# Part of the last projection block moved between attention's first scores, with a new instruction order for the attention stage

## Chip, cores and metric

The kernel runs on one core of one Trainium2 chip. A core has TensorE (PE), VectorE (DVE), ScalarE (ACT), GpSimd (POOL) and SyncE (SP), which issues most DMAs. The metric is device microseconds of one launch; less is better.

## What is computed

One inference step of a decoder with two layers, for a prompt of 1024 tokens and 8 x 4 = 32 sample tokens, 1056 in all, width 1024, in float32. Layer 0 projects x to 3352 columns that feed two branches. Layer 1 is a pooling mixer. The change touches layer 0 alone, cut here to what matters:

```python
h = jnp.einsum('btd,de->bte', x, w_in)
a_val, a_glu, a_gate, q, kv_c, kv_s, kv_w, g, b_gate = jnp.split(h, offsets, axis=-1)
u = a_val * jax.nn.sigmoid(a_glu)
# branch A: causal depthwise convolution of width 31, layer norm over channels, gates
a_out = jax.nn.silu(layer_norm(y, ln_g, ln_b)) * jax.nn.silu(a_gate)
# branch B: attention over compressed blocks, the 16 best blocks and a window of 512
o = gq[..., 0:1] * o_c + gq[..., 1:2] * o_s + gq[..., 2:3] * o_w
h = jnp.concatenate([a_out, b_out * jax.nn.silu(b_gate)], axis=-1)
y = jnp.einsum('bte,ed->btd', h, w_out)
x = layer_norm(alpha * x + y)
```

The 32 sample tokens attend to 2048 cached keys each, fetched page by page, and their block choice depends on their compressed scores.

## The kernel before

**Projection.** `one(m)` computes block m of 27 (m = 0 to 26), 128 columns of `w_in` for all tokens. Weights are loaded to WRAW, split by ACT into a high part WH (`high`), and by DVE or POOL into the rest WL (`low`). PE makes 72 matmuls of 352 columns per block (line 728): 8 slices of the contraction, three products (XH with WH, XL with WH, XH with WL), three column thirds. `evac(m)` on ACT takes the result out of three PSUM banks, 0 to 2 for even m, 3 to 5 for odd. Block 22 holds the attention gates G, blocks 23 to 26 the quarters of `b_gate` (BG), with a SiLU.

**Statistics.** The layer norm of branch A runs beside blocks 24 and 25. `mean(c)` and `variance(c)` (lines 763 to 772) are matmuls of PE with a constant matrix, put between the block's slices; DVE centres, adds squares and normalises (lines 648 to 677), ACT squares and takes the root, and afterwards applies SiLU to Y (line 494). POOL then multiplies Y by the gate AG (line 357). Before block 24 PE transposes the gates G (line 836), which ACT copies to GTOK (line 483).

**Values.** After block 26 PE transposes the value rows of KV (lines 852 and 858), and ACT and DVE copy them to TM (lines 501 and 680).

**Attention.** For each of 48 units (query tile, head pair, branch) there are two pairs p: `S` scores on PE (line 1334) into banks 0 to 3, `M` masks and takes the least on DVE (line 1432), `E` is the exponential on ACT (line 1377), `R` the reciprocal on DVE (line 1428), `C` the scaling on POOL (line 1589). `T` are turns of the probabilities by PE into banks 4 and 5 (line 1195), which DVE and ACT copy to PT (lines 1367 and 1371), and `V` multiplies them by the values into bank 6 (line 1213). `H` and `cast` split Y for the output product (lines 1533 and 1617).

**Samples.** One bank, 7, serves the samples' steps one after another: `csc`, compressed scores (line 1226); `cmax`, `cexp`, `cnorm`; `gs`, sums over heads (line 1234), from which `rank` on DVE chooses blocks (lines 1463 to 1469); `kt`, turned key tiles (line 1251); `sc` and `scw`, scores (line 1257), taken by DVE; `pt` and `pv`, the values' product (line 1310). Selected keys come by gathers of POOL's queue into RING (line 1574), window rows by SP's queue (line 1621). `dve_queries` fills QBD, `pool_prep` and `dve_prep` the small columns TI, NEWM, NM4 and WM4.

**Order.** The order of all this on each engine comes from a planner that runs when the program is built. It holds a list of steps with durations and lags in ns, simulates them, and takes at each point the step with the largest remaining path plus a constant per engine and kind:

```python
begin = max([now[e] + (SWITCH if mode != pe_mode and e == "PE" else 0)] + [end[y] + lag for y, lag in after])
may.append((begin, remains[x] + PREFER.get((e, kind), 0), kind, x))
```

Of the kernel before, what the change touches and what calls it, by code (L numbers as in the profile page):

```python
# [72 lines left out]
def program(nc, x_prompt, x_sample, cache_kv_cmp, cache_kv_sel, state_win_kv, state_conv, state_pool, page_table,  # L73
# [4 lines left out]
    with ctx:  # L78
# [61 lines left out]
        EPSC = const("EPSC", [P, 1])  # L140
        assert cur[0] <= 206016 + 6368, cur[0]
# [48 lines left out]

        def values_copied(eng):

            eng.wait_ge(s_tma, 3)
            eng.wait_ge(s_tmv, 2)

        def value_rows(n):

            out = TM[:, 2 * n:2 * n + 2, 256:768].rearrange("p t (a c) -> p t a c", a=2)[:, :, :, P:2 * P]
            return out, PS[:, 3 + n, :].rearrange("p (t a c) -> p t a c", t=2, a=2)
# [35 lines left out]
        def sp_program(sp):  # L235
# [36 lines left out]
            sp.wait_ge(s_tmt, 5)  # L272
# [26 lines left out]
        def pool_program(po):  # L299
# [50 lines left out]
            for m in range(LOW_DVE[1], NM + 1):  # L350
                po.wait_ge(s_wl, m)
                low(po, m)
            po.wait_ge(s_mean, 3)
            pool_masks(po, link)
            for i in range(4):
                po.wait_ge(s_ys, i + 1)
                po.tensor_tensor(Y[:, i, :], Y[:, i, :], AG[i][:, :], ALU.mult).then_inc(s_ya, 1)
            po.wait_ge(s_ya, 4)
# [3 lines left out]
        def act_program(act):  # L362
# [6 lines left out]
            def high(m):  # L369
                act.wait_ge(s_raw[m % 2], raw_need[m])  # L370
                if m >= 2:
                    act.wait_ge(s_mm, m - 1)
                n = width(m)
# [14 lines left out]
            def evac(m):  # L388
                b0 = 3 * (m % 2)
# [68 lines left out]
            for m in range(NM + 1):  # L458
# [38 lines left out]
            for n in (0, 2):  # L497
                act.wait_ge(s_tmt, n + 1)
                act.activation(*value_rows(n), ACT.Copy).then_inc(s_tma, 1)
            act.wait_ge(s_tmt, 5)  # L500
            act.activation(TM[0:NSAMP, 8, 384:768], PS[0:NSAMP, 7, 0:384], ACT.Copy).then_inc(s_tma, 1)
# [3 lines left out]
        def dve_program(v):  # L505
# [159 lines left out]

            centre(0)
# [11 lines left out]
            for n in (1, 3):  # L678
# [5 lines left out]
        def pe_program(pe):  # L684
# [154 lines left out]
            pe.wait_ge(s_gtok, 1)  # L839
            pe.wait_ge(s_ev, 2 + 24)  # L840
# [3 lines left out]
            one(NM)  # L844


            pe.wait_ge(s_ev, 2 + NM)
            for n in range(5):
# [4 lines left out]
                else:  # L853
                    if n == 3:
                        pe.wait_ge(s_stdc, 3)
                    for t in range(2):
                        for a in range(2):
                            ins = pe.transpose(PS[:, 3 + n, (2 * t + a) * P:(2 * t + a) * P + P], KV[:, 3 + 2 * a, tok(2 * n + t)],
                                               ident[:, :])
                ins.then_inc(s_tmt, 1)  # L860
# [1502 lines left out]
```

## Time and profile before

| | |
|---|---|
| median of 3 runs | 1101.97 us (1101.74 to 1102.1) |
| the profiled execution | 1101.45 us |
| its span, first to last instruction | 1099.7 us |
| mean granted TensorE clock | 0.991 |
| PE busy | 1052.6 us, 96% |
| DVE busy | 744.4 us, 68% |
| ACT busy | 381.9 us, 35% |
| POOL busy | 364.8 us, 33% |
| projection | to 389 us |
| attention | 391 to 676 us |

PE stands for the matmuls, PEld for the loading of weights into the array. Busy time of PE is modelled from starts, since matmuls overlap. A row's bracket tells how long the engine was idle just before it, and what ended the wait.

### The profile page before, as it was taken

What the parts mean: (1) busy time and instruction counts of PE and PEld (TensorE: products, weight loads), DVE (VectorE), ACT (ScalarE), POOL (GpSimd) and SP (SyncE); (2) the same over time, 40 slices, a digit from 0 to 9 for tenths busy, and PEclk for the clock granted to TensorE, in tenths of its full rate; (3) what the DMA queues carried; (4) which work ended last, traced back from release to release, by engine and by line L of the source; (5) the groups of instructions that cost most, each with busy time, mean ns of one, the idle gap of its engine ahead of it and who ended that gap; (6) DMA issues with size and microseconds to landing.
All of it is one profiled execution on the core that took longest, in us unless ns stands there. A gap on an engine that the chain in (4) does not pass through costs nothing.

```text
span 1099.7 us, 18908 instructions
## 1 busy us (share of the span) xinstructions
PE 1052.6 (96%) x7604; PEld 893.4 (81%) x7604; DVE 744.4 (68%) x1377; ACT 381.9 (35%) x805; POOL 364.8 (33%) x379
## 2 busy tenths in 40 slices
PE   6998999999999988999999999999999999999997
PEld 5888999999998954666655566887899999998875
DVE  3677889999888776776666666766555720257755
ACT  3211111212322554887566855311111211344000
POOL 3544530000101486665883562400032221308000
PEclk9999999999999988999999999999999999999998
DMA  8655421152322035300771046622221111042321
GB/s 238 218 165 172 130 96 45 39 197 80 111 41 43 1 107 173 117 2 1 269 266 43 2 169 203 173 100 75 77 77 57 38 57 45 1 153 77 134 82 63
DMA packets 85888, 113.73 MB, mean 103 GB/s; under 512 B 21952, under 2 KB 67144, under 8 KB 85727
## 3 DMA queue, kind: packets, MB, share of 16 engines
q1 hardware_dynamic: 71849, 69.51, 20.6%
q0 software_dynamic: 11776, 41.95, 11.0%
q10 hardware_dynamic: 2182, 1.16, 0.4%
q8 instruction: 55, 0.90, 0.3%
q14 instruction: 26, 0.21, 0.1%
HBM read 100.91 MB, written 16.64 MB: 107 GB/s over the span
## 4 chain that ended last, share of the span: by engine, by line
PE 84%; DVE 6%; DMA 3%; issue 2%; ACT 2%; POOL 1%; SPq 0%; DVEq 0%; POOLq 0%
PE PS L728 26%; PE PS L2079 16%; PE PS L1847 14%; PE PS L1213 5%; PE PS L1334 5%; PE PS L1195 4%; PE PS L716 3%; PE PS L1871 2%; DMA WRAW<-in_w_in_even 2%; PE PS L1251 2%; PE PS L1860 1%; DVE ACC L569 1%; DMA TM<-in_state_win_kv 1%; PE PS L2059 1%; PE PS L1310 1%
## 5 line engine op out<-in xcount | busy, mean ns | idle before, releaser
L616 DVE SCALAR_TENSOR_TENSOR Y<-U,SM,Y 128x1024 f32<-128x1024 f32 x120 | 150.1, 1312 | 0.3
L728 PE MATMUL PS<-XH,WH 128*128 128x352 f32 (+1 forms) x648 | 146.1, 330 | 1.8 <-ACT GTOK L483 1.8
L728 PE MATMUL PS<-XL,WH 128*128 128x352 f32 (+1 forms) x648 | 143.6, 326 | 0.0
L728 PE MATMUL PS<-XH,WL 128*128 128x352 f32 (+1 forms) x648 | 142.9, 325 | 0.0
L728 PEld LDWEIGHTS PS<-XH,WH 128*128 128x128 f32 (+1 forms) x648 | 107.5, 185 | 4.2 <-issue 1.9
L728 PEld LDWEIGHTS PS<-XH,WL 128*128 128x128 f32 (+1 forms) x648 | 107.9, 185 | 1.4
L728 PEld LDWEIGHTS PS<-XL,WH 128*128 128x128 f32 (+1 forms) x648 | 107.7, 185 | 1.4
L2186 POOL TENSOR_TENSOR WL<-WRAW,WH 128x1024 fp32r<-128x1024 f32 x14 | 37.5, 2675 | 208.7 <-ACT WH L2131 208.7
L569 DVE SCALAR_TENSOR_TENSOR ACC<-PS,SM,ACC 128x508 f32<-128x508 f32 x124 | 86.9, 742 | 25.1 <-PE PS L716 23.1
L2079 PE MATMUL PS<-XH,WH 128*128 128x352 f32 x360 | 77.2, 323 | 0.0
L2079 PE MATMUL PS<-XH,WL 128*128 128x352 f32 x360 | 77.1, 323 | 0.0
L2079 PE MATMUL PS<-XL,WH 128*128 128x352 f32 x360 | 77.1, 322 | 0.0
L1334 PE MATMUL PS<-KV,Q 64*128 64x512 f32 (+3 forms) x384 | 75.7, 482 | 0.4 <-DVE STAT L1432 0.4
L1213 PE MATMUL PS<-PT,TM 128*64 128x256 f32 x528 | 73.1, 399 | 1.2 <-DVE BG L1528 1.2
L1847 PE MATMUL PS<-WOH,XH 128*128 128x512 f32 x224 | 71.0, 398 | 0.0
L1847 PE MATMUL PS<-WOL,XH 128*128 128x512 f32 x224 | 69.8, 393 | 0.0
L1847 PE MATMUL PS<-WOH,XL 128*128 128x512 f32 x224 | 69.5, 391 | 0.0
L1589 POOL TENSOR_SCALAR PRS<-PRS,STAT,GTOK 128x512 f32<-128x512 f32 (+7 forms) x64 | 52.0, 826 | 32.9 <-DVE STAT L1428 32.7
L1367 DVE COPY PT<-PS 128x512 f32<-128x512 f32 (+1 forms) x80 | 51.6, 645 | 15.8 <-PE PS L1213 8.7
L1334 PEld LDWEIGHTS PS<-KV,Q 64*128 64x128 f32 x384 | 38.4, 186 | 29.4 <-issue 15.8
L2079 PEld LDWEIGHTS PS<-XH,WL 128*128 128x128 f32 x360 | 61.0, 188 | 0.0
L2079 PEld LDWEIGHTS PS<-XL,WH 128*128 128x128 f32 x360 | 60.9, 188 | 0.0
(339 smaller groups left out, 2002.2 us busy)
## 6 DMA issues: line engine op xcount, KB each, us to landing
WRAW<-in_w_in_even SPq DMA_DIRECT2D x16, 512.0 KB, 3.8
WRAW<-in_w_in_odd SPq DMA_DIRECT2D x16, 512.0 KB, 4.0
TM<-in_state_win_kv SPq DMA_DIRECT2D x12, 512.0 KB, 6.6
XIN<-in_x_prompt SPq DMA_DIRECT2D x8, 512.0 KB, 15.7
WRAW<-in_w_in_even SPq DMA_DIRECT2D x16, 256.0 KB, 3.7
XR<-in_x_prompt SPq DMA_DIRECT2D x8, 512.0 KB, 3.5
layer_out<-R SPq DMA_DIRECT2D x8, 512.0 KB, 2.7
XR<-layer_out SPq DMA_DIRECT2D x8, 512.0 KB, 3.2
```

Source lines behind the costliest of these rows:

```text
L569: ins = v.scalar_tensor_tensor(acc, rows, weight, acc, ALU.mult, ALU.add)
L616: v.scalar_tensor_tensor(dst, src, CWT[:, i, t:t + 1], dst, ALU.mult, ALU.add).then_inc(s_cv, 1)
L716: ins = pe.transpose(PS[:, 6 + x, b * P:b * P + P], XC[:, load % 2, b, 256 * j + P * x:256 * j + P * x + P], ident[:, :])
L728: ins = pe.matmul(PS[0:mcols, 3 * slot + c, 0:CH], w[:, slot, kk, 0:mcols], x[:, kk, c * CH:(c + 1) * CH], start=(kk == 0 and n == 0), sto ...
L1195: ins = pe.transpose(PS[0:rows, 4 + a, c:c + 64], x[half, :], ident[half, half])
L1213: ins = pe.matmul(PS[hb:hb + HD, 6, 256 * gp:256 * gp + 256], v, PT[k % 2][0:rows, j, 256 * h:256 * h + 256], start=first, stop=(br == CMPB))
L1334: ins = pe.matmul(PS[:, row_bank[j] + b // 512, 0:w], Q[hb:hb + HD, g, tok(qt)], keys[:, k0 + b:k0 + b + w], start=True, stop=True)
L1367: ins = copy(out[:, :, :, a, :], PS[0:rows, 4 + a, 0:256 * k].rearrange("p (t x q) -> p t x q", t=k, q=64))
L1589: po.tensor_scalar(x, x, RCP[:, stat(p, h):stat(p, h) + 1], GTOK[:, qt, c:c + 1], ALU.mult, ALU.mult)\
L1847: ins = pe.matmul(PS[0:n, b0 + hf, :], x[:, kk, tok(tile)], w[:, kk, hf * 512:hf * 512 + 512], start=(kk == 0 and i == 0), stop=(kk == KT ...
L2079: ins = pe.matmul(PS[:, b0 + c, 0:CH], w[:, slot, kk, :], x[:, kk, c * CH:(c + 1) * CH], start=(kk == 0 and n == 0), stop=(kk == KT - 1 an ...
L2186: po.tensor_tensor(WL[:, m % 2, :, :], WRAW[:, m % 2, :, :], WH[:, m % 2, :, :].bitcast(F32), ALU.subtract).then_inc(s_wl2, 1)
```

## The change

- Block 26 is no longer made by `one`. Its high and low parts are made in two and three pieces, the half of slices 4 to 7 first, into the other weight slot (WHX) and into WLX. PE makes slices 4 to 7 behind the turned values, and the planner places the other twelve groups, `D`, each three matmuls. Its result goes to banks 4 to 6, and its evacuation is a step of the planner, `gate`.
- The values are turned ahead of block 26, into banks 0 to 3 and 7, and DVE makes all five copies.
- The waits for GTOK and for block 23's evacuation go from before block 24 to the means 1 and 2.
- `pool_prep` and `dve_prep` run during the statistics, into tiles of their own. The query columns are made by POOL, after the masks.
- Two of four gating products are steps of the planner. The casts, the samples' maximum and the window loads wait for block 26.
- The planner has new durations, models DMAs as an engine, and a second table of constants by eighths of each kind's line.

```diff
-            pe.wait_ge(s_gtok, 1)
-            pe.wait_ge(s_ev, 2 + 24)
             one(24, ((2, mean, 0), (2, mean, 1), (2, mean, 2), (6, variance, 0)))
...
-            one(NM)
...
+            def last_block(kk, n):
+                high = last_high((0, 4))[:, kk, :] if kk < 4 else last_high((4, 8))[:, kk - 4, :]
+                low = last_low((0, 4))[:, kk, :] if kk < 4 else last_low((kk // 2 * 2, 0))[:, kk % 2, :]
+                w, x = ((high, XH), (high, XL), (low, XH))[n]
+                for c in range(3):
+                    ins = pe.matmul(PS[:, LAST_BANK + c, 0:CH], w, x[:, kk, c * CH:(c + 1) * CH],
+                                    start=(kk == 4 and n == 0), stop=(kk == 3 and n == 2))
+                return ins
...
+            pe.wait_ge(s_wl, NM + 1)
+            pe.wait_ge(s_ev, 2 + NM)
+            pe.wait_ge(s_stdc, 3)
+            for kk in range(4, KT):
+                for n in range(3):
+                    last_block(kk, n)
+            pe_attention(pe, last_block)
...
+                if c == 1:
+                    pe.wait_ge(s_gtok, 1)
+                elif c == 2:
+                    pe.wait_ge(s_ev, 2 + 24)
...
+            pool_prep(po, link)
-            for m in range(LOW_DVE[1], NM + 1):
+            for m in range(LOW_DVE[1], NM):
...
+            for kks in ((4, 6), (6, 8), (0, 4)):
...
+            pool_queries(po, link)
...
+            for i in range(2):
+                gated(i)
+            pool_attention(po, link, gated)
...
+            dve_prep(v, link)
             centre(0)
...
-            for n in (1, 3):
+            v.wait_ge(s_wl, NM + 2)
+            for n in range(VALUES):
...
-            sp.wait_ge(s_tmt, 5)
+            sp.wait_ge(s_mm, NM + 1)
             sp_windows(sp, 0)
...
-        PE_END, SOON, FREED, VALUES_READ, LANDS = 205, 140, 190, 315, 5500
+        PE_END, SOON, FREED, VALUES_READ, LANDS = 205, 140, 190, 315, 400
...
-        SWITCH, NEAR = 150, 150
+        SWITCH, NEAR = 95, 150
...
+        for i in range(12):
+            step("PE", "D", ("D", i), 482, mode=WHOLE)
+        step("ACT", "B", ("gate",), 3600, (("D", 11), PE_END))
+        for i in range(2, 4):
+            step("POOL", "G", ("gated", i), 2430)
...
             step("POOL", "X", ("gather", a, q, b), 1250, *after)
+            step("DMA", "L", ("land", a, q, b), 1700, (("gather", a, q, b), 1200))
...
-        step("DVE", "X", ("prep2",), 1100, (("prep",), 130))
...
-                            may.append((begin, remains[x] + PREFER.get((e, kind), 0), kind, x))
+                            may.append((begin, remains[x] + PREFER.get((e, kind), 0) + PREFER_EIGHTH.get((e, kind, done), 0), kind, x))
```

Where the instructions stand. On PE, from the end of block 26 to the first turn of probabilities, in the kernel before (KV with Q are scores, KCTS the samples' compressed scores, ident with PRS the turn):

```order
L728 MATMUL PS<-XH,WL 128x352 x3
L858 MATMUL PS<-ident,KV 128x128 x16
L852 MATMUL PS<-ident,KV 32x128 x3
L1334 MATMUL PS<-KV,Q 128x512 x4
L1226 MATMUL PS<-KCTS,QBD 32x127 x8
L1334 MATMUL PS<-KV,Q 128x512 x4
L1334 MATMUL PS<-KCT,Q 128x63 x4
L1334 MATMUL PS<-KV,Q 128x512 x2
L1195 MATMUL PS<-ident,PRS 128x64 x16
```

and in the changed kernel from the first two scores on (line 882 is `last_block`, 1397 the scores):

```order
L1397 MATMUL PS<-KV,Q 128x512 x4
L882 MATMUL PS<-XH,WL 128x352 x3
L882 MATMUL PS<-XH,WH 128x352 x3
L882 MATMUL PS<-XL,WH 128x352 x3
L882 MATMUL PS<-XH,WL 128x352 x3
L882 MATMUL PS<-XH,WH 128x352 x3
L882 MATMUL PS<-XL,WH 128x352 x3
L882 MATMUL PS<-XH,WL 128x352 x3
L1397 MATMUL PS<-KV,Q 128x512 x4
L1290 MATMUL PS<-KCTS,QBD 32x127 x8
L1397 MATMUL PS<-KCT,Q 128x63 x2
L1259 MATMUL PS<-ident,PRS 128x64 x16
```

Seven groups of block 26 stand between the first two and the next two scores, five more ahead of the first, and the first turn follows fewer scores.

On DVE, ahead of the samples' choice of blocks (MAX and MATCH_REPLACE are its first steps), before:

```order
L1428 RECIPROCAL STAT<-STAT 128x2
L1645 TENSOR_SCALAR TI<-TI 128x1
L1646 CAST SE<-TI 128x1
L1647 CAST SE<-TI 128x4
L1648 TENSOR_SCALAR SE<-SE 128x4
L1649 TENSOR_SCALAR SE<-SE 128x4
L1651 TENSOR_TENSOR NEWM<-NEWM,SE 128x64
L1428 RECIPROCAL STAT<-STAT 128x2
L1463 MAX TM<-TM 128x8
L1464 MATCH_REPLACE LEFT_SCORES<-TM 128x30
```

and in the changed kernel:

```order
L1525 TENSOR_REDUCE TM<-PS 128x32 x2
L1529 TENSOR_SCALAR TM<-TM,STAT 128x128 x2
L1537 MAX TM<-TM 128x8
L1538 MATCH_REPLACE LEFT_SCORES<-TM 128x30
L1539 MAX TM<-LEFT_SCORES 128x8
L1540 MEMSET TM 128x3
L1541 MATCH_REPLACE LEFT_SCORES<-TM,LEFT_SCORES 128x30
L1542 TENSOR_SCALAR TM<-LEFT_SCORES 128x30
L1543 COPY TM<-TM 128x128
L1537 MAX TM<-TM 128x8
```

The small columns (TI, SE, NEWM) are gone from here, and the choice of blocks follows the group sums directly.

On POOL, from the last gating product to the first scalings (PRS), before:

```order
L357 TENSOR_TENSOR Y<-Y,AG_58 128x1056
L1617 CAST XH<-Y 128x1056 x2
L1574 DMA RING<-in_cache_kv_sel,idx 128x1024
L1617 CAST XH<-Y 128x1056
L1589 TENSOR_SCALAR PRS<-PRS,STAT,GTOK 128x512 x4
L1589 TENSOR_SCALAR PRW<-PRW,STAT,GTOK 128x512 x4
L1589 TENSOR_SCALAR PRC_106<-PRC_106,STAT,GTOK 128x63
```

and in the changed kernel:

```order
L1708 MEMSET QBD 128x256
L1711 COPY QBD<-Q 64x8x16 x2
L381 TENSOR_TENSOR Y<-Y,AG_55 128x1056
L381 TENSOR_TENSOR Y<-Y,AG_56 128x1056
L381 TENSOR_TENSOR Y<-Y,AG_57 128x1056
L381 TENSOR_TENSOR Y<-Y,AG_58 128x1056
L1644 DMA RING<-in_cache_kv_sel,idx 128x1024
L1659 TENSOR_SCALAR PRS<-PRS,STAT,GTOK 128x512 x4
L1644 DMA RING<-in_cache_kv_sel,idx 128x1024 x3
L1689 CAST XH<-Y 128x1056 x2
L1659 TENSOR_SCALAR PRW<-PRW,STAT,GTOK 128x512 x2
```

The query columns QBD are ahead of the gating now, and the casts behind the first scaling.

## Rows read from the trace of the kernel before

**Rows 1.** Page: busy time by engine, and the chain of waits by engine.

```profile
PE 1052.6 (96%) x7604; PEld 893.4 (81%) x7604; DVE 744.4 (68%) x1377; ACT 381.9 (35%) x805; POOL 364.8 (33%) x379
...
PE 84%; DVE 6%; DMA 3%; issue 2%; ACT 2%; POOL 1%; SPq 0%; DVEq 0%; POOLq 0%
```

**Rows 2.** Busy time by stretch: PE, PEld, DVE, ACT, POOL, granted clock, DMA.

```profile
391.00:420.00 29.00, 19.69 (x121) 10.51 (x118) 25.96 (x92) 15.14 (x44) 22.42 (x29) 0.85 0.49 156
420.00:484.00 64.00, 62.25 (x651) 38.76 (x649) 43.89 (x200) 49.04 (x158) 43.14 (x72) 0.96 0.30 100
484.00:560.00 76.00, 72.54 (x892) 47.16 (x893) 51.95 (x200) 54.06 (x158) 55.18 (x78) 1.00 0.39 131
560.00:676.00 116.00, 112.81 (x1333) 70.11 (x1331) 75.91 (x217) 81.31 (x185) 63.55 (x76) 1.00 0.35 121
```

**Rows 3.** PE in order of time, around the gates' transposes: start, length, what, idle before.

```profile
348.30 0.70 PE L836 MATMUL PS<-ident,G 24*128 24x24 f32 x9
350.77 0.72 PE L728 MATMUL PS<-XH,WH 128*128 128x352 f32 x3 [1.77 <-ACT GTOK L483]
```

**Rows 4.** Chain of waits in order of time, one projection block.

```profile
251.45 11.56 PE PS L728 x72
```

**Rows 5.** PE in order of time, 389 to 421 us.

```profile
389.04 1.91 PE L858 MATMUL PS<-ident,KV 128*128 128x128 f32 x16
...
391.20 1.99 PE L1334 MATMUL PS<-KV,Q 64*128 64x512 f32 x8
...
400.03 0.67 PE L1195 MATMUL PS<-ident,PRS 64*128 64x64 f32 x14
...
403.99 0.68 PE L1234 MATMUL PS<-TM,GSM 128*128 128x128 f32 x4 [2.25 <-DVE TM L1447]
...
419.12 1.11 PE L1251 MATMUL PS<-ident,RING 128*128 128x128 f32 x4 [4.47 <-DVE LOW L1432]
420.17 1.11 PE L1195 MATMUL PS<-ident,PRW 64*128 64x64 f32 x16
```

**Rows 6.** DVE in order of time, 378 to 420 us.

```profile
378.26 1.83 DVE L677 TENSOR_TENSOR Y<-Y,RSTD 128x352 f32<-128x352 f32 x4
390.11 0.69 DVE L680 COPY TM<-PS 128x512 f32<-128x512 f32 x1 [10.02 <-PE PS L858]
...
393.61 0.69 DVE L1432 CUSTOM_DVE_ANT_0 PRS<-PS,MASKC 128x512 f32<-128x512 f32 x1
...
412.50 0.15 DVE L1645 TENSOR_SCALAR TI<-TI 128x1 int32<-128x1 int32 x1 [1.31 <-POOL NEWM L1663]
...
414.51 0.17 DVE L1463 MAX8 TM<-TM 128x8 f32<-128x30 f32 x1
...
418.18 0.16 DVE L1497 TENSOR_TENSOR PS<-PS,SE 64x4 f32<-64x4 f32 x1
```

**Rows 7.** POOL in order of time, 380 to 400 us.

```profile
380.18 9.74 POOL L357 TENSOR_TENSOR Y<-Y,AG 128x1056 f32<-128x1056 f32 x4 [3.68 <-ACT Y L494]
391.43 2.08 POOL L1617 CAST XH<-Y 128x1056 fp32r<-128x1056 f32 x2 [1.51 <-PE PS L852]
393.66 1.02 POOL L1574 DMA_INDIRECT RING<-in_cache_kv_sel,idx  x1 [0.16 <-issue]
...
396.33 3.04 POOL L1589 TENSOR_SCALAR PRS<-PRS,STAT,GTOK 128x512 f32<-128x512 f32 x4 [0.58 <-DVE STAT L1428]
```

**Rows 8.** ACT in order of time, a table load and an evacuation.

```profile
369.63 1.28 ACT L426 ACT_TABLE_LOAD   x1
370.93 1.05 ACT L426 ACTIVATE BG<-PS 128x1056 f32<-128x1056 f32 x1
```

**Rows 9.** Busy time by stretch, the two stretches at the lower clock.

```profile
407.00:411.00 4.00, 4.00 (x29) 2.41 (x28) 3.35 (x9) 2.75 (x8) 3.53 (x4) 0.50 0.56 151
...
419.00:425.00 6.00, 5.88 (x48) 3.97 (x48) 2.53 (x5) 1.79 (x3) 2.97 (x4) 0.50 0.32 88
```

**Rows 10.** Page: issues of the selected-key gathers, KB, median us to landing.

```profile
RING<-in_cache_kv_sel,idx POOLq DMA_INDIRECT x48, 5.8
```

More of the change, by code:

```diff
@@ L372, in high @@
                     act.wait_ge(s_mm, m - 1)
+                if m == NM:
+                    act.wait_ge(s_wl, m)
+                    for kks in ((4, 8), (0, 4)):
+                        act.activation(last_high(kks), WRAW[:, 0, kks[0]:kks[1], :], ACT.Copy).then_inc(s_wh, 1)
+                    return
                 n = width(m)
@@ L456, in past @@
                     .then_inc(s_vcn, 1)
-            for m in range(NM + 1):
+            for m in range(NM):
                 evac(m)
@@ L495, in act_program @@
                             .then_inc(s_ys, 1)
[L497 to L501, printed above, removed]
+            act_attention(act, evac)
             act_late(act)
@@ L968, in program @@
         PV_PARTS = 6
-        PE_END, SOON, FREED, VALUES_READ, LANDS = 205, 140, 190, 315, 5500
+        PE_END, SOON, FREED, VALUES_READ, LANDS = 205, 140, 190, 315, 400
         BY_ROWS, WHOLE, BY_QUARTERS, BY_HALVES = "64 rows", "128 by 128", "32 columns", "64 columns"
-        SWITCH, NEAR = 150, 150
-        todo, about = {e: {} for e in ("PE", "DVE", "ACT", "POOL")}, {}
+        SWITCH, NEAR = 95, 150
+        todo, about = {e: {} for e in ("PE", "DVE", "ACT", "POOL", "DMA")}, {}
         def step(engine, kind, what, ns, *after, mode=None):
@@ L983, in turn @@
         def turn(kind, what, blocks, after, copied):
-            step("PE", kind, what, 62 * blocks, *after, mode=BY_ROWS)
+            step("PE", kind, what, 62 * blocks + 20, *after, mode=BY_ROWS)
             step("ACT", "P", ("ACT", what), 72 + 52 * blocks, (what, PE_END), *copied)
@@ L1023, in copied @@
             return (("ACT", x), SOON), (("DVE", x), SOON)
-        fill(("csc",), 430, (("queries",), SOON))
-        step("DVE", "X", ("cmax",), 900, (("csc",), PE_END))
+        fill(("csc",), 640)
+        step("DVE", "X", ("cmax",), 900, (("csc",), PE_END), (("D", 11), PE_END))
         step("ACT", "X", ("cexp",), 750, (("cmax",), 100))
@@ L1031, in program @@
         take("DVE", ("gs",), 1500)
-        fill(("pct",), 220, (("take", ("gs",)), SOON), mode=WHOLE)
+        fill(("pct",), 330, (("take", ("gs",)), SOON), mode=WHOLE)
         take("ACT", ("pct",), 380)
@@ L1035, in gather, with windows @@
             step("POOL", "X", ("gather", a, q, b), 1250, *after)
+            step("DMA", "L", ("land", a, q, b), 1700, (("gather", a, q, b), 1200))
+        def windows(n, *after):
+            step("DMA", "W", ("windows", n), 3400, *after)
         for b in range(4):
-            gather(0, 0, b)
-        step("POOL", "X", ("prep",), 1300)
+            gather(0, 0, b, (("gated", 3), 100))
         for b in range(4):
             gather(0, 1, b, (("H", 3), 100))
-        step("DVE", "X", ("prep2",), 1100, (("prep",), 130))
         for a in range(2):
@@ L1137, in program @@
                 for kind, line in todo[e].items():
+                    done = 8 * (lines[e, kind] - len(line)) // lines[e, kind]
                     for x in line[:1] if kind != "P" else [y for y in line if y[1] == turned_last[0]]:
@@ L1411, in act_attention @@
                     exponential(*ev[1:])
+                elif ev[0] == "gate":
+                    evac(NM)
                 elif ev[0] == "ACT":
```

140 lines of the change are left out of this document (81 added, 59 removed), and 4 rows, old and new, of the table PREFER_EIGHTH.

## The prediction

> **What bounds the kernel now.** I read the page's shares first: PE is busy for 96% of the span and carries 84% of the chain of waits [rows 1]. So the kernel is TensorE's work plus its holes, and a change that adds no matmul can only win holes or clock. Next I cut the span into stretches, to find the holes [rows 2]. Of the 29 us from 391 to 420, the opening of attention, PE is busy for 19.7, so 9.3 us are holes, at a mean granted clock of 0.85; DVE is busy for 26.0 there. The 256 us that follow hold only 1.8 + 3.5 + 3.2 = 8.4 us of holes. The change works on the worst place and, through the new order, on all the rest.
>
> In order of time the opening reads thus. The last projection block ends at 389.04, the values are turned until 391.20, scores begin, and the first turn of probabilities comes at 400.03 [rows 5]. Two waits of PE are then for the samples' small steps on DVE: 2.25 us, and 4.47 us before the first gathered key tile [rows 5]. What DVE does in the second is: the small columns at 412.50, which wait 1.31 us for POOL, then both rankings from 414.51 to 418.18, and only then the window scores that free the bank [rows 6]. The clock answers: from 407 to 411 and from 419 to 425 it is granted at 0.50, that is 1.2 GHz in place of 2.4, with PE busy for 4.0 and 5.9 us [rows 9]. At half speed that loses 2.0 + 2.9 = 4.9 us. Both stretches follow a hole.
>
> **The change, edit by edit.**
>
> The gates' wait. PE stands 1.77 us before block 24 for the gates' copy [rows 3]. The changed kernel moves this wait and that for block 23's evacuation to the second and third means, nine matmul groups and more later, when both have come. All the statistics follow PE by that amount, so 1.8 us are won. The small columns go to the time between the channel sums and the centring. DVE's part took about 1.9 us, from 412.50 to the ranking at 414.51 less one reciprocal [rows 6]; DVE has to wait there for the mean anyway, and at most 0.5 us of it shows, before a variance that PE takes later than it is ready. I cost it at nothing; without that cover it would cost 1.9.
>
> Values ahead of the block. Block 25 ended at 389.04 less one block of 11.56 [rows 4, 5], 377.5; now 375.7. The turns take the same 2.2 us: 377.9. DVE now makes all five copies. Its normalising ended at 380.1 [rows 6], now 378.3, and five copies of at most 0.69 end at 381.8. PE does the block's first half meanwhile, 11.56 / 2 = 5.8, to 383.7, so the copies are hidden with 1.9 us to spare. The low parts of the weights on POOL are the same elements in three pieces, and they are done while block 25 runs.
>
> The second half between the scores. Five of its twelve groups (0.48 each) come first: 386.1. Then two scores (2.0 [rows 5]): 388.1. Seven groups: 391.5. Two scores: 393.5; samples' compressed scores and one small score, 1.0: 394.5, and the turn. Is the turn ready? It needs POOL's two scalings. POOL's gating of Y took 9.74 us from 380.18 [rows 7]. It could start 1.8 us sooner, but the query columns now stand ahead of it on POOL. No row shows them on POOL: two copies of 128 columns cost between 0.13 each (a cast of 1056 took 1.04 [rows 7], by length) and the 1.0 of the whole cast. I take 0.7, nearer the cast, since short strided copies don't scale by length; gating then starts at 380 as before and ends by 389.9. One gather, 1.2: 391.1. From the first score to the first scaling took 396.33 - 391.20 = 5.1 us [rows 5, 7], which gives 386.1 + 5.1 = 391.2. Two scalings, 3.0: 394.2. The gate's evacuation on ACT, with a table load, 1.28 + 1.05 [rows 8], ends at 393.9 and frees the banks of the turn. Three paths meet at 394.5, against 400.03 before.
>
> The table loads are two more, in the middle of the exponentials. The row shows the evacuation starting 1.30 us after the load's start [rows 8]; the load back costs the same, and delays the samples' exponential by about that, which I have counted. The Trainium skill (ScalarE: Activation LUTs, "What ACT_TABLE_LOAD costs") gives about 1.28 us for the load, which the row bears out, and 1.38 us of drain on top, which no row here shows; by it the samples' chain would end 2.8 us later and the time would be some 1093.8 us.
>
> The opening behind the first turn. Before, the turn of the window probabilities at 420.17 is where the last hole has closed [rows 5]. I walk to the same turn. DVE does three more maskings (0.62 apart [rows 6]), the samples' maximum and norm, and takes the group scores at about 400.4. Both rankings follow at once, 3.7: 404.1. Then reciprocals and three maskings, 3.0, and the copy of the second turn, 0.7: 407.8, and PE turns at 408.1. PE has some 4 us of holes from 399 to 408 where it had 9.3 from 391 to 420. That is 12.1 us sooner, but one score (1.0) and one key tile (0.5) that stood ahead now stand behind: 10.6 won, the 1.8 of the first edit among them, and 2.0 of the clock.
>
> The clock. With 4 us of holes in nine, I expect one stretch at half speed to remain, just behind, at the mean of the two seen, 2.5 us; the second, 2.9, goes. That is 0.4 more: 11.0. Bounds: none remains (2.5 more), or both do (2.9 less).
>
> The rest of the order. The other 250 us are ordered anew; PE does the same work. Its holes there are 8.4 us. They can't all go and could grow: I take no change, with 3 us either way, about the largest of the three stretches' sums [rows 2]. One wait moves: the second quarter of gathered keys is let go by the fourth low cast on DVE, about 421 as before, while PE arrives 10 us sooner. The rows of the first key tile of that quarter come five turns and five score groups behind 408, at some 427; a gather is 1.0 us of POOL and lands 5.8 us from its issue [rows 10]: just in time.
>
> Sum against the profiled execution's 1101.45 us: - 11.0 = 1090.5. The median of the runs shown lies 0.5 above the profiled one, so 1091.0.
>
> **Rivals.**
>
> A. The clock never drops, since the block's full-width matmuls fill the opening, and the new order also trims the rest: 1091.0 - 2.5 - 1.5 = 1087. For it: the drops followed holes of 2.3 and 4.5 us [rows 5], and of mine only one reaches 2. Against: they add up to 4 us in nine. 17%.
>
> B. The opening only slides. The holes of the samples' chain stay as they were, because the first turn waits for POOL all the same and DVE's queue is as full (26.0 of 29). Only 1.8, and what the earlier turn wins, remain: 5.5 less two small scores now behind it (1.4) = 4.1, to 1097. For it: POOL ends its gating when it did. 13%.
>
> C. Slower. The new order counts a gather as landed 3.3 us after its issue (1.2 + 1.7 + 0.4), the old one counted 5.5 behind an instruction of 1.25; the median here is 5.8 [rows 10]. Twelve groups of four tiles wait for gathers. If PE stands 2.5 us at each, that is 30 - 11 = 19 us slower, 1121; it decides from 0.9 us a group on. Against: the four gathers share the queue, and the order counts 1.7 us for each of them in a line, so that the last lands late in its count too. 6%.
>
> D. It doesn't do what it says: the two halves cover nothing, since PE had no hole before 400 (the holes lie behind). Then only 1.8 us are won, and the reordering gives or takes the rest: 1100. 4%.
>
> **How the numbers follow.** My forecast, 1088 to 1094, has 60%. The range takes in A's time and the lower bound less one us, 1086, and B's, 1097; C, D and what lies under 1086 are left out, together below 2 in 10. 0.2%, 2.2 us, is about what a measurement of this kernel tells from no change. Faster by more: 60 + 17 + 13 = 0.90. Within: 0.04, D. Slower: 0.06, C.
>
> **What would show it.** In the changed kernel's profile: no wait of PE for the gates' copy; turns of the values before 378; the second half's matmuls around the first two scores; the first turn at 394 to 395; one stretch of 0.50 clock or none; the window turn at about 408; holes of the opening near 4 us, of the rest near 8. If the first turn comes at 397 or later, POOL's query columns or the gate's evacuation were dearer. If PE's waits name gathers, C holds.

## The result, and the profile after

| | before | changed |
|---|---|---|
| median of 4 runs, us | 1102.03 (1101.74 to 1102.33) | 1089.58 (1087.41 to 1090.44) |
| profiled execution, us | 1101.45 | 1089.39 |
| its span, us | 1099.7 | 1087.6 |
| mean granted clock | 0.991 | 0.992 |

The ratio is 0.9884, 95% interval 0.9867 to 0.9901. The forecast of 1091.0 us is 1.4 us above the median, and the range holds it. As will be seen, two of its parts were off and nearly cancelled: the opening won less than I walked through, the rest more. That the number came so close is in part luck.

PE in order of time in the changed kernel, against [rows 3, 5]:

```profile
351.54 0.75 PE L799 MATMUL PS<-SIG,meanm 128*128 128x352 f32 x2
...
375.56 1.96 PE L897 MATMUL PS<-ident,KV 128*128 128x128 f32 x16
...
385.97 1.99 PE L1397 MATMUL PS<-KV,Q 64*128 64x512 f32 x8
...
391.45 1.99 PE L1397 MATMUL PS<-KV,Q 64*128 64x512 f32 x8
...
394.21 0.70 PE L1259 MATMUL PS<-ident,PRS 64*128 64x64 f32 x16
...
399.94 0.68 PE L1298 MATMUL PS<-TM,GSM 128*128 128x128 f32 x4 [2.24 <-DVE TM L1519]
...
403.55 0.69 PE L1304 MATMUL PS<-ident,TM 128*128 128x128 f32 x2
404.71 1.11 PE L1315 MATMUL PS<-ident,TM 128*128 128x128 f32 x4 [0.47 <-ACT TM L1440]
406.51 1.12 PE L1315 MATMUL PS<-ident,TM 128*128 128x128 f32 x4 [0.69 <-ACT KTS L1440]
...
411.41 0.78 PE L1259 MATMUL PS<-ident,PRW 64*128 64x64 f32 x14
```

Up to 394.2 this is the walk of the prediction to within 0.3 us: first scores 385.97 (386.1 forecast), first turn 394.21 (394.5). Behind it a hole of 2.24 us stands before the group scores, and the window turn comes at 411.41, not 408.1. Busy time by stretch, cut at the same pieces of work as [rows 2] and at the slow clock [rows 9] (PE, PEld, DVE, ACT, POOL, granted clock, DMA):

```profile
386.00:411.00 25.00, 20.89 (x132) 11.46 (x131) 19.70 (x75) 16.95 (x44) 20.47 (x24) 0.81 0.48 159
...
475.00:551.00 76.00, 72.63 (x875) 46.73 (x873) 52.14 (x175) 53.30 (x141) 49.39 (x67) 0.98 0.32 110
...
401.00:411.00 10.00, 8.84 (x30) 3.17 (x26) 8.81 (x36) 4.39 (x11) 7.37 (x11) 0.53 0.29 99
538.00:542.00 4.00, 4.00 (x53) 2.68 (x55) 0.94 (x2) 0.84 (x2) 3.11 (x4) 0.57 0.43 124
```

The opening holds 4.1 us of holes, as forecast, but ten microseconds run at about half the clock, and there is a new slow stretch at 538. The 12.06 us between the two profiled executions lie so: 8.8 by the window turn (420.17 to 411.41), 1.8 from there to the output product (676.44 to 665.83), 1.5 behind it, where nothing was changed. The last is chance: in a second profile of the changed kernel (further below) the part from the output product on takes 423.5 us, as in the kernel before (423.2), and not 421.8.

What makes the hole of 2.24 us is seen on DVE and POOL. DVE, one and the same operation on the two halves of the samples' probabilities:

```profile
396.74 2.66 DVE L1519 TENSOR_SCALAR TM<-TM,SE 128x127 f32<-128x127 f32 x1
...
399.51 0.29 DVE L1519 TENSOR_SCALAR TM<-TM,SE 128x127 f32<-128x127 f32 x1
...
401.43 1.30 DVE L1529 TENSOR_SCALAR TM<-TM,STAT 128x128 f32<-128x128 f32 x2
```

POOL at that time:

```profile
378.28 0.98 POOL L1711 COPY QBD<-Q 64x128 f32<-64x128 f32 x2
379.45 9.70 POOL L381 TENSOR_TENSOR Y<-Y,AG 128x1056 f32<-128x1056 f32 x4 [0.19 <-POOL QBD L1711]
...
390.51 3.04 POOL L1659 TENSOR_SCALAR PRS<-PRS,STAT,GTOK 128x512 f32<-128x512 f32 x4
...
396.27 0.95 POOL L1644 DMA_INDIRECT RING<-in_cache_kv_sel,idx  x1 [0.30 <-issue]
397.22 2.09 POOL L1689 CAST XH<-Y 128x1056 fp32r<-128x1056 f32 x2
...
401.59 2.07 POOL L1689 CAST XH<-Y 128x1056 fp32r<-128x1056 f32 x2
```

The first took 2.66 us, the second 0.29, and the first ends when POOL's two casts do (399.31). Its first 0.48 us lie beside the issue of a gather, which ends where the casts begin; the order had put both beside it. The pair of L1529, beside the next two casts, takes 1.30 us, where the kernel before took 0.48 (L1457, at 405.45). The new hole at 538 has the same face. PE, DVE, and then POOL:

```profile
537.86 0.99 PE L1259 MATMUL PS<-ident,PRS 64*128 64x64 f32 x16 [2.40 <-POOL PRC L1659]
```

```profile
533.68 2.64 DVE L1498 TENSOR_SCALAR STAT<-STAT 128x2 f32<-128x2 f32 x1
...
536.75 0.16 DVE L1498 TENSOR_SCALAR STAT<-STAT 128x2 f32<-128x2 f32 x1
```

```profile
532.85 3.44 POOL L1659 TENSOR_SCALAR PRW<-PRW,STAT,GTOK 128x640 f32<-128x640 f32 x4
536.62 1.59 POOL L1659 TENSOR_SCALAR PRC<-PRC,STAT,GTOK 128x63 f32<-128x63 f32 x4 [0.33 <-DVE STAT L1499]
```

Two numbers per partition take 2.64 us beside POOL's scalings (532.85 to 536.29), and 0.16 when these are over; POOL then waits for the reciprocal behind it, and PE for POOL. The long one did not get in between POOL's scalings, which follow each other without a gap, about 0.86 us each. Nor does every overlap cost as much: the one of 0.16 runs beside POOL's next, shorter scalings, and the median of the 32 of L1498 is 0.20. On this the Trainium skill (SBUF — State Buffer, "Terms") says that DVE and GpSimd share a pair of SBUF ports, held for a whole instruction, and that the loser blocks fully. The rows agree: the long one ends with the other engine's instruction. The experiments test whether POOL is the cause.

### The profile page after: what moved, and what is told of

Its sections match the earlier page's. It is cut to its first block, busy times and chain, and to the rows that moved or that the text cites. A ratio compares the mean times of both kernels' runs of the same rounds, so it can differ in the third digit from the quotient of the medians.

```text
span 1087.6 us, 18920 instructions
## 1 busy us (share of the span) xinstructions
PE 1047.4 (96%) x7604; PEld 887.9 (82%) x7604; DVE 750.5 (69%) x1377; ACT 382.2 (35%) x805; POOL 368.0 (34%) x384
## 4 chain that ended last, share of the span: by engine, by line
PE 87%; DVE 5%; DMA 3%; issue 2%; ACT 2%; POOL 1%; SPq 0%; DVEq 0%
PE PS L758 25%; PE PS L2150 16%; PE PS L1918 14%; PE PS L1397 6%; PE PS L1277 5%; PE PS L1259 3%; PE PS L746 3%; PE PS L1942 2%; PE PS L1315 2%; DMA WRAW<-in_w_in_even 2%; PE PS L1931 1%; PE PS L1374 1%; DVE ACC L597 1%; DMA RING<-in_cache_kv_sel,idx 1%; PE PS L2130 1%
## 5 line engine op out<-in xcount | busy, mean ns | idle before, releaser
L758 PE MATMUL PS<-XH,WH 128*128 128x352 f32 (+1 forms) x624 | 141.1, 330 | 0.0
L758 PE MATMUL PS<-XL,WH 128*128 128x352 f32 (+1 forms) x624 | 138.7, 326 | 0.0
L758 PE MATMUL PS<-XH,WL 128*128 128x352 f32 (+1 forms) x624 | 137.8, 325 | 0.0
L758 PEld LDWEIGHTS PS<-XH,WH 128*128 128x128 f32 (+1 forms) x624 | 103.4, 185 | 2.4
L758 PEld LDWEIGHTS PS<-XH,WL 128*128 128x128 f32 (+1 forms) x624 | 103.9, 185 | 1.4
L758 PEld LDWEIGHTS PS<-XL,WH 128*128 128x128 f32 (+1 forms) x624 | 103.7, 185 | 1.4
L2150 PEld LDWEIGHTS PS<-XH,WH 128*128 128x128 f32 x360 | 60.9, 188 | 0.0
```

Source lines behind the costliest of these rows:

```text
L758: ins = pe.matmul(PS[0:mcols, 3 * slot + c, 0:CH], w[:, slot, kk, 0:mcols], x[:, kk, c * CH:(c + 1) * CH], start=(kk == 0 and n == 0), sto ...
L2150: ins = pe.matmul(PS[:, b0 + c, 0:CH], w[:, slot, kk, :], x[:, kk, c * CH:(c + 1) * CH], start=(kk == 0 and n == 0), stop=(kk == KT - 1 an ...
```

## The experiments

The ratios are to runs of the kernel before on the same chip (medians of 1101.58 to 1102.54 us).

**The gates' wait alone**, in the kernel before.

```diff
-            pe.wait_ge(s_gtok, 1)
-            pe.wait_ge(s_ev, 2 + 24)
...
+                if c == 1:
+                    pe.wait_ge(s_gtok, 1)
+                elif c == 2:
+                    pe.wait_ge(s_ev, 2 + 24)
```

> The kernel before, with only the wait for the gates' copy (and for block 23's evacuation) moved from before block 24 to the second and third mean. Theory: PE gains the 1.77 us that it stood there and nothing takes it up, so 1.8 us faster (1100.2), the first scores 1.8 us sooner. Rival: POOL and DVE set the opening of attention, the gain is met by a hole further on: within 0.5 us of before.

1099.09 us (1096.91 to 1099.71, 11 runs), ratio 0.9978 (0.9965 to 0.9991): 2.8 us by the medians, 2.6 by the profiled executions (1098.89). Nearly all of it has happened by the window turn: 417.8 against 420.17. But the gates' transposes, ahead of the edit, already start at 347.82 and not 348.30. From them to the samples' compressed scores it is 43.5 us against 45.3: the term is 1.8, as I had it, and the other 0.5 came from ahead of the change.

**The second half in one piece ahead of the scores**, in the changed kernel.

```diff
+            for i in range(12):
+                ins = last_block(i // 3, i % 3)
+            ins.then_inc(s_mm, 1)
             for ev in order["PE"]:
...
                 elif ev[0] == "D":
+                    continue
```

> The changed kernel, with all twelve groups of the last block ahead of the first score instead of five ahead and seven between; the rest of the order is kept. Theory: the scores start the chain to the first turn (5.1 us to POOL's first scaling, 3.0 for two scalings), so the first turn comes about 3 us later (397.5 in place of 394.2) and the kernel is 2 to 3.5 us slower than the changed one. Rival: POOL's gating (to 389.2) sets the first turn anyway, or the holes behind absorb it: less than 0.7 us slower.

1091.52 us (1089.43 to 1091.75, 5 runs), ratio 0.9912 (0.989 to 0.9933). The first turn comes at 396.4 and not 394.2, the window turn at 411.9, half a microsecond behind. By the medians, letting scores in between is worth 1.9 us against the first runs of the changed kernel and 3.3 against the repeat below; the interval overlaps that of the first and only touches that of the repeat, so the size stays rough. One profile can't give it either: the half-speed stretches of its opening add up to 7 us, where those of the changed kernel's two profiles are of 10 and 3.4.

**The old constants**, in the changed kernel: `PREFER` as before and no table by eighths.

```diff
-        PREFER = {("ACT", "P"): 362000, ("ACT", "X"): -10000, ("DVE", "H"): -257000, ("DVE", "M"): -38000, ("DVE", "O"):
...
+        PREFER = {("ACT", "P"): 15000, ("ACT", "X"): -19000, ("DVE", "H"): -90000, ("DVE", "P"): -11000, ("DVE", "W"):
...
+        PREFER_EIGHTH = {}
```

> The changed kernel, with the planner's old constants per kind and without the second table by eighths; durations, lags and all steps as changed. Theory: the structure (block 26 in the opening, values ahead, small columns early) brings most, and the constants 2 to 5 us of the 12: 1091.5 to 1095. Rival 1: the constants bring nothing on the chip (within 1 us of the changed kernel). Rival 2: without them the plan is worse than before (above 1102).

1103.8 us (1101.42 to 1105.6, 12 runs), ratio 1.0021 (1.0008 to 1.0035): all of the gain is lost, and a little more. PE in order of time there:

```profile
390.45 1.99 PE L1393 MATMUL PS<-KV,Q 64*128 64x512 f32 x8
...
396.42 0.43 PE L1393 MATMUL PS<-KCT,Q 64*128 64x63 f32 x2 [0.97 <-DVE STAT L1499]
...
402.34 1.11 PE L1255 MATMUL PS<-ident,PRS 64*128 64x64 f32 x16 [2.42 <-POOL PRS L1655]
```

The whole second half goes ahead of the first score, the first turn comes at 402.3, later than before the change, and by the output product the kernel is 2.6 us behind the kernel before. With the old constants the structure wins nothing; it needs an order that uses it.

**The plan alone**, in the kernel before: all of the planner's new durations, DMAs and constants, without the steps of the last block and the gating.

```diff
-        PE_END, SOON, FREED, VALUES_READ, LANDS = 205, 140, 190, 315, 5500
+        PE_END, SOON, FREED, VALUES_READ, LANDS = 205, 140, 190, 315, 400
-        SWITCH, NEAR = 150, 150
+        SWITCH, NEAR = 95, 150
...
+            step("DMA", "L", ("land", a, q, b), 1700, (("gather", a, q, b), 1200))
```

> The kernel before, unchanged but for the planner: the changed kernel's durations, lags, DMA steps, constants and table by eighths, without the steps for block 26, its evacuation and the gating. The constants were not made for this list of steps. Theory 1, plan and structure depend on each other: the run with the old constants lost all of the gain (1103.8), so the new plan alone gains little too, 1097 to 1102. Theory 2, the plan is the gain: 1090 to 1094, and the structure is worth what the gates' wait gives, 2 to 3 us. Theory 3, the plan alone is slower than before: above 1103.

1095.21 us (1093.02 to 1097.24, 6 runs), ratio 0.9942 (0.9927 to 0.9958): 6.4 us, half of the whole gain. The window turn is only 1.5 us sooner (418.7), the output product 4.6 (671.8). It already has the hole of 2.4 us before a turn (543 us), and its opening runs at half speed for some 14 us, from 401 to 415.

**The small columns early**, in the kernel before.

```diff
+            pool_prep(po, link)
             for m in range(LOW_DVE[1], NM + 1):
...
+            dve_prep(v, link)
             centre(0)
```

> The kernel before, with the small columns made on POOL and DVE during the statistics and taken out of attention; the plan still counts them, so no order changes. Theory: DVE's 1.31 us of waiting and 1.9 of work stand before the rankings and so in PE's hole of 4.47 us, which shrinks by about 3.2 us to 1.3; the kernel is 2.5 to 3.5 us faster than before, more if the second stretch of the lower clock (419 to 425) goes with the hole. Rival: the hole only moves, since the rankings wait for POOL's or ACT's steps next: less than 1 us.

1099.13 us (1097.19 to 1102.72, 11 runs), ratio 0.998 (0.997 to 0.999): 2.4 us. PE's wait before the gathered key tile is 2.52 us in place of the 4.47 of [rows 5]:

```profile
417.75 0.66 PE L1254 MATMUL PS<-ident,RING 128*128 128x128 f32 x4 [2.52 <-DVE LOW L1435]
```

This profile also has a stretch at half speed that the kernel before's hasn't, behind the same wait of 1.77 us for the gates' copy (granted clock 0.58 from 350 to 354, against 1.00 from 351 to 355). It cost 1.5 us ahead of attention: the first mean comes 7.0 us behind the gates' transposes and not 5.5. So the move may be worth more than 2.4 where this does not happen.

The three parts by themselves give 2.8 + 2.4 + 6.4 = 11.6 us, and all together 12.4 in the first runs, 13.4 in the repeat below. If they simply added, 1 to 2 us would be left for the values and the halved block, the part that names the change. That they add is not shown: the kernel with the old constants holds the first two parts as well, 5.2 us, and shows none of it. What the values and the halved block are worth stays open; the second experiment prices one piece, the scores in between, at some 2 to 3 us.

**POOL's casts held back**, the first two until DVE has normalised the samples' probabilities, the last two until it has scaled them for the group sums (L1529).

```diff
+                    po.wait_ge(s_pcn, 2 if i < 2 else 4)
                     po.tensor_copy(XH[:, i, :], Y[:, i, :]).then_inc(s_ah, 1)
```

> The changed kernel, with POOL's first two casts of Y waiting for the samples' norm on DVE and the last two for the group sums' product. In the changed kernel's profile DVE's 127-wide product takes 2.66 us at 396.74 and ends with POOL's two casts (397.22 to 399.31), where the same product takes 0.29 just behind. Theory: DVE stands for the port it shares with POOL. Then the product takes 0.3 us here, the group sums come about 2.2 us sooner (398), PE's hole of 2.24 us goes, and the kernel is 1.5 to 3 us faster than the changed one. Rival 1: the product is slow for another cause, stays above 2 us, and nothing changes. Rival 2: it is short, but the casts come later, DVE's low parts and the gathers behind them too, and the time is given back: within 0.7 us or slower.

1087.65 us (1085.92 to 1091.9, 4 runs), ratio 0.9872 (0.9846 to 0.9898), not told apart from the changed kernel. But L1519 takes 0.44 (beside a gather's issue, and ending with it) and 0.29 us, and the group scores start at 398.6 in a run whose start was 0.9 later. The casts now meet the rankings:

```profile
402.21 1.09 DVE L1542 TENSOR_SCALAR TM<-LEFT_SCORES 128x30 f32<-128x30 f32 x1
403.33 1.02 DVE L1543 COPY TM<-TM 128x128 f32<-128x128 f32 x1
...
405.54 0.18 DVE L1542 TENSOR_SCALAR TM<-LEFT_SCORES 128x30 f32<-128x30 f32 x1
405.75 0.23 DVE L1543 COPY TM<-TM 128x128 f32<-128x128 f32 x1
```

1.7 us of blocking have moved by some microseconds, to the chain that leads to the window turn; PE waits 2.12 us there for DVE's masks.

**The hole filled with matmuls**, to test whether the slow clock behind it costs what was won.

```diff
+                if ev == ("gs",):
+                    for _ in range(4):
+                        pe.matmul(PS[:, 6, 0:CH], meanm[:, :], KV[:, 2, 0:CH], start=True, stop=True)
```

> The changed kernel, with four extra matmuls of 352 columns (about 2 us of PE, results unused) put into PE's hole of 2.24 us before the samples' group sums, at 397.7. Theory: the clock falls at 401.8 because of the holes since 395.1; with that filled it stays at 1.00 through most of 402 to 411, and the kernel is 2 to 4 us faster although it works more. Rival: the clock falls a few us later all the same, after the holes at 404 and 406, for the same length: no gain, or the 0.3 us that the matmuls overhang is lost.

1091.8 us (1090.57 to 1093.62, 5 runs), ratio 0.9911 (0.9897 to 0.9924). It is 3.6 us slower than the changed kernel's repeat, which ran beside it (next), and the intervals don't meet. The half-speed stretch starts at 408 and not 401 and lasts 7 us, the window turn is at 411.3, and another stretch stands at 664. At 539, where PE has its hole of 2.3 us as before, the clock stays full this time. The clock is granted differently and nothing is won: that theory fell. What the rest of the 3.6 us is stays open.

**The changed kernel again.**

> The changed kernel once more, so that the runs of this call have it on their own chip: 0.986 to 0.990 of before, and 1087 to 1090.5 us.

1088.21 us (1086.66 to 1090.11, 4 runs), ratio 0.9875 (0.986 to 0.989). In its profile the half-speed stretch in the opening lies between 399 and 404 only, and the window turn is at 410.0:

```profile
399.00:404.00 5.00, 4.46 (x18) 2.01 (x18) 4.44 (x18) 1.22 (x8) 3.54 (x4) 0.66 0.69 271
```

A mean of 0.66 over 5 us is half speed for 3.4. The same kernel, with the same hole before the group scores (within 0.1 us), was thus granted half speed for about 3.4 microseconds or for ten. This alone doesn't order its runs, which lie within 3.8 us: this execution, with the shorter stretch, took 1090.11 us, the other 1089.39.

**The normalising from PSUM.** Instead of moving either instruction, this changes the form: the exponentials stay in bank 7.

```diff
-                        act.activation(PC[:, a, 0:NCS], PS[:, 7, a * P:a * P + NCS], ACT.Exp, bias=ENM[:, a:a + 1], scale=SCALE,
+                        act.activation(PS[:, 7, a * P:a * P + NCS], PS[:, 7, a * P:a * P + NCS], ACT.Exp, bias=ENM[:, a:a + 1], scale=SCALE,
...
-                        v.wait_ge(s_cex, a + 1)
+                        v.wait_ge(s_cex, 2)
...
-                        v.tensor_scalar(PC[:, a, 0:NCS], PC[:, a, 0:NCS], ERC[:, a:a + 1], None, ALU.mult).then_inc(s_pcn, 1)
+                        v.tensor_scalar(PC[:, a, 0:NCS], PS[:, 7, a * P:a * P + NCS], ERC[:, a:a + 1], None, ALU.mult).then_inc(s_pcn, 1)
```

> The changed kernel, but the exponentials of the samples' compressed scores stay in bank 7 of PSUM and the DVE's TENSOR_SCALAR of L1519 reads them there, so that it no longer has both operands in SBUF (the first of the pair waits for the second exponential too, 0.3 us more). Theory (the 2.66 us of L1519 are a wait for the SBUF port that POOL's cast of 2.09 us holds): L1519 takes about 0.2 to 0.4 us, the group scores start near 397.5 instead of 399.9, the hole of 2.24 us before them falls to under 0.5, and the time falls by 0.5 to 2 us, as with the casts made to wait. Rival (the instruction is slow for a reason of its own, or POOL holds the DVE up whatever it reads): L1519 still shows over 2 us and the time stays within 0.5.

1090.06 us (1087.73 to 1092.01, 5 runs), ratio 0.989 (0.9871 to 0.9909). The mechanism is shown, the gain is not there. L1519 now takes 0.35 us both times, beside the same gather (396.48 to 397.43) and the same casts (from 397.44):

```profile
396.93 0.35 DVE L1519 TENSOR_SCALAR TM<-PS,SE 128x127 f32<-128x127 f32 x1
397.39 0.35 DVE L1519 TENSOR_SCALAR TM<-PS,SE 128x127 f32<-128x127 f32 x1
```

The hole before the group scores is gone (they start at 397.88, no wait). But the rankings, 2 us sooner, now meet the second pair of casts, and their TENSOR_SCALAR takes:

```profile
401.67 1.49 DVE L1542 TENSOR_SCALAR TM<-LEFT_SCORES 128x30 f32<-128x30 f32 x1
```

**The floor by a reduction.** The other blocked instruction, the floor under the softmax sums of the compressed branch, gets a form that reads a sum and the constant beside it.

```diff
+            v.memset(DENF[:, :], 1e-30)
...
+                d = DENF[:, 2 * c:2 * c + 4].rearrange("p (h k) -> p h k", k=2)
+                r = RCP[:, c:c + 2]
...
-                    link(v.tensor_scalar(d, d, 1e-30, None, ALU.max))
+                    link(v.tensor_reduce(r, d, AX, ALU.max))
```

> The changed kernel, but the floor of 1e-30 under the softmax sums of the compressed branch (L1498, a TENSOR_SCALAR of 128x2 in SBUF, 32 of them, mean 0.38 us, one of 2.64 us beside POOL's scalings at 533.7 ahead of the 2.4 us hole at 538) is a TENSOR_REDUCE over the sum and a constant beside it. Theory (the port): no instruction of that line shows over 0.5 us, the hole before the turn at 538 falls from 2.4 to under 0.6 us, the half-speed stretch behind it (538 to 541) goes or is shorter, and the time falls by 2 to 4 us. Rival (the hole is POOL's own lateness, its scalings being the last of a queue): the long instruction goes, the hole stays above 1.5 us, time within 0.7.

1086.27 us (1083.54 to 1088.66, 5 runs), ratio 0.9855 (0.9834 to 0.9875): 3.3 us under the changed kernel's first median, 1.9 under its second, with an interval that overlaps both. Beside the same scalings of POOL (534.64 to 538.07 in this run) the new instruction takes:

```profile
535.52 0.15 DVE L1501 TENSOR_REDUCE STAT<-DENF 128x2 f32<-128x4 f32 x1
...
536.23 0.16 DVE L1501 TENSOR_REDUCE STAT<-DENF 128x2 f32<-128x4 f32 x1
```

The hole at 538 and the slow stretch behind it are gone. At 431 a wait of 2.05 us for a gather stands where the changed kernel waited 0.16, with a slow stretch of its own behind it. The group scores' hole and ten microseconds at half speed in the opening are as they were.

**Both forms.**

> The changed kernel with both of the above. Theory: both holes go, and the time falls by the sum, 2.5 to 5 us, to 1084 to 1087. Rival: as the changed kernel, within 1 us.

1087.0 us (1083.84 to 1088.57, 4 runs), ratio 0.9856 (0.9834 to 0.9877). No more than the floor alone. The rival for this run, no gain over the changed kernel, is not quite ruled out: 1.2 us under the repeat's median, with intervals that overlap. The opening shows why: L1547, the rankings' TENSOR_SCALAR, takes 1.50 us beside the casts, and PE stands for the masks that DVE makes behind the rankings:

```profile
406.64 2.07 PE L1399 MATMUL PS<-KV,Q 64*128 64x512 f32 x2 [1.78 <-DVE STAT L1508]
...
410.49 1.12 PE L1261 MATMUL PS<-ident,PRW 64*128 64x64 f32 x16
```

**Both forms, and the last two casts behind the rankings.**

```diff
                     po.wait_ge(s_ya, i + 1)
+                    if i >= 2:
+                        po.wait_ge(s_rank, 2)
```

> The kernel with both forms changed, and POOL's third and fourth cast wait until the two rankings are done. In the run with both forms the first ranking's TENSOR_SCALAR (L1547) took 1.50 us against 0.18 for its twin, beside those casts, and the matmuls of the sixth score pair waited 1.78 us for the masks behind the rankings. Theory (the port again, and the rankings are on the path to the window turn): that instruction takes 0.2 us, the masks come 1.3 us sooner, the hole of 1.78 us falls to about 0.5, the window turn is at 409 to 409.5 instead of 410.5, and the time falls by about 1 us, to 1085.5 to 1086.5. Rival (the path there is PE's own order at its granted clock, or the second pair of window probabilities, which POOL now scales behind the casts, is late): the hole goes, the window turn stays at 410.2 or later, and the time stays at 1087 or rises.

1083.8 us (1082.85 to 1086.25, 5 runs), ratio 0.9838 (0.982 to 0.9857). All five runs lie below all eight of the changed kernel, and its interval meets neither of that kernel's two; it is the fastest version here. Against both forms without the held casts it is 3.2 us less by the medians, where I had expected about 1, but these two intervals overlap. PE in order of time:

```profile
394.46 0.70 PE L1261 MATMUL PS<-ident,PRS 64*128 64x64 f32 x16
...
397.94 0.68 PE L1300 MATMUL PS<-TM,GSM 128*128 128x128 f32 x4
...
405.18 1.12 PE L1399 MATMUL PS<-KV,Q 64*128 64x512 f32 x2 [0.55 <-DVE STAT L1508]
406.23 1.05 PE L1323 MATMUL PS<-KTS,QBD 128*32 128x512 f32 x4
407.62 0.71 PE L1261 MATMUL PS<-ident,PRW 64*128 64x64 f32 x16 [0.34 <-POOL PRW L1664]
```

Busy time by stretch:

```profile
386.00:410.00 24.00, 21.24 (x161) 11.86 (x159) 19.06 (x80) 17.55 (x45) 20.09 (x22) 1.00 0.57 188
...
474.00:550.00 76.00, 75.55 (x911) 48.42 (x909) 51.61 (x183) 56.70 (x146) 53.76 (x71) 1.00 0.41 141
```

The blocked instruction of the rankings takes 0.18 us, the window turn comes at 407.6, and the clock is full throughout attention. The first turn is where it was in the changed kernel (394.46 and 394.21). So the 3.8 us between its window turn and this one (counted from the gates' transposes in each run 4.1, and 3.0 against the second profile) are DVE's blocked time and the slow clock behind it; the two are not told apart by these runs.

What the table by eighths gives by itself, apart from the new constants per kind, was not measured.

## Why the prediction was right, and where it was not

- **The gates' wait, 1.8.** Right: 2.6 to 2.8 alone, of which 1.8 behind the edit itself.
- **The small columns at nothing.** Nearly right. From the gates' transposes to the turned values the changed kernel won 1.5 us of the 1.8 (29.2, with block 26's 11.56 taken off, to 27.7), so that at most 0.3 shows, though the work was longer than the 1.9 us I gave it: from 350.78 to the centring at 353.81, 3.0 us, because DVE's cast of L1719, which took 0.50 us in the kernel before, took 2.08 beside POOL's subtraction of 350.15 to 353.09, again ending with it. No wait of PE is listed for it. What they held up in the old place is 2.4 us, by moving them alone.

```profile
351.04 2.08 DVE L1719 CAST TABLES<-TI 128x4 f32<-128x4 int32 x1
```

- **Values and halved block, first turn at 394.5.** Right, 394.21, though all of it stands 0.4 us earlier by chance (the gates' transposes start at 347.89 and not 348.30). The query columns on POOL took 0.98 us for both copies, which I had at 0.7, and a memset of 0.31 besides; gating ended at 389.15 and not 389.9. DVE's five copies took 2.93 us and were hidden. But what it is worth was never priced by itself, and the runs leave it open.
- **The table loads.** The way back takes, on ACT:

```profile
393.30 1.28 ACT L1446 ACT_TABLE_LOAD   x1
394.60 0.72 ACT L1446 ACTIVATE PRW<-PRW,STAT 128x512 f32<-128x512 f32 x1
```

  1.30 us from load to next activation. The drain on top that the Trainium skill gives (ScalarE: Activation LUTs, "What ACT_TABLE_LOAD costs") shows in no row, and the measured time is 4 us under the 1093.8 that it would have made.
- **The opening behind the first turn: the step that failed.** "DVE does three more maskings ..., and takes the group scores at about 400.4", then the rankings to 404.1 and the turn at 408.1. Each instruction was given its undisturbed time, as if DVE and POOL never got in each other's way. One was blocked for 2.4 us; the group sums reached DVE at 401.1, L1529 took 1.30 in place of 0.48, the rankings ran from 402.8 to 406.0, and the turn came at 411.4. So 1.9 of the 3.3 us were lost by the end of the rankings, and 1.4 behind them, where PE ran at half speed. In the last experiment, without the blocking of L1519 and of the rankings, the turn is at 407.6. The walk was partly lucky there: it left no time for summing and scaling ahead of the rankings (0.8 us in the kernel before, 405.11 to 405.93) and gave the rankings 3.7 where they took 3.2.
- **The clock.** "One stretch at half speed, 2.5 us lost." It was one in the opening, but of ten microseconds (8.84 us of PE's busy time x 0.47 = 4.2 lost), and a second one at 538 (4.00 x 0.43 = 1.7). The second profile, with 3.4 us in the opening, comes nearer to the forecast there, so the size of this term is chance as much as error. I had also read the stretches of the kernel before too short: the clock was at 0.61 from 404 to 407 already, so that they lost 2.9 us each and not 2.0 and 2.9.
- **The rest of the order, 0 within 3.** The window turn gave 12.1 - 8.8 = 3.3 us less than the walk. From there to the output product I had a loss of 1.5 - 0.4 = 1.1 (work moved, less the clock), and 1.8 were won: 2.9 more, inside the 3 either way. Behind the output product 1.5 came that I hadn't counted, by luck, since the second profile doesn't have it. Together 2.9 + 1.5 - 3.3 = 1.1, the distance of the profiled execution (1089.39) from the 1090.5 of the sum. The plan alone, at 6.4 us, was the largest part, and I had given it no term.
- **Rivals.** A's clock that never drops came true only in the last experiment, at 1083.8. B (only a slide) had the wait right that stayed, the 2.24 us of the samples' chain, but the wrong cause. C is refuted: after the window turn PE waits for gathers 1.6 us in all (1.2 + 0.4). D is refuted by the first scores at 386. Two figures there were off by themselves: B's 1097 is on the scale of the profiled execution and would be 1097.9 as a median, and with both slow stretches left the loss would be 2.4 and not 2.9.

## To carry to other kernels

Where a row shows an instruction ten times longer than its twin, look at what POOL runs in that moment and whether the two end together. If so, change the form of the short one (PSUM as source, a reduction for an element-wise operation), which helps wherever the planner puts it, or hold the long one behind the whole chain of short ones. Moving it a little only moves the collision. And take a change of structure and its new order apart before crediting either: here the order alone gave half, and the structure with the old constants gave nothing.

## What the runs showed of the hardware

DVE's TENSOR_SCALAR of 128x2, 128x30, 128x127 and its CAST or COPY of 128x4 and 128x128, SBUF to SBUF, took up to 2.64, 1.50, 2.66, 2.08 and 1.02 us beside POOL's instructions, against 0.16, 0.18, 0.29, 0.50 and 0.23 elsewhere. The longest waits span several instructions of POOL in a row: a gather's issue and two casts, or three scalings. POOL can be the one that waits: in the kernel before a scaling of PRW took 1.78 us (400.84 to 402.62) beside DVE's subtraction L1533 (400.21 to 401.98), the next one 0.77. In the same stretches RECIPROCAL (0.17), the TENSOR_REDUCE of the floor (0.15), the TENSOR_SCALAR from PSUM (0.35) and copies from PSUM (0.69) kept their times. The Trainium skill (SBUF — State Buffer, "SBUF: two separate sides") limits the lock to DVE's two-port modes and to operations with two SBUF inputs; the forms that were held up and those that were not are in line with that here. An instruction of two elements per partition can so cost PE 2.4 us, where the profile names POOL as what PE waited for and only the row of DVE ahead shows the length.

TensorE's granted clock of the same program with the same holes differed from run to run: in the opening 1.2 GHz for ten microseconds in one and about 3.4 in the other. Behind the gates' wait of 1.77 us the clock stayed full in the kernel before and fell in the run with the small columns early; behind the hole of 2.3 us at 538 it fell in both profiles of the changed kernel and stayed full in the run with four added matmuls, which moved the opening's stretch and did not pay. Only the version without the hole before the group scores, the one at 538 and the long wait for the masks kept 2.4 GHz throughout attention, in its one profile, and it has holes left, one of 1.64 us at 655.5 and this:

```profile
426.30 0.63 PE L1317 MATMUL PS<-ident,RING 128*128 128x128 f32 x4 [1.21 <-DMA RING<-in_cache_kv_sel,idx]
```
